# A new order of VectorE and ScalarE work in the paged-attention stage, with page numbers read ahead of the slot wait

## The reference

```python
q, k, v, c_in = split(u)                      # 8 heads; two score maps per head
# group A, samples: keys and values of 2048 past tokens come in pages of 128 tokens
k_past = cache_k[page_table]                  # (8 samples, 16 pages, 128 tokens, 8 heads, 128)
v_past = cache_v[page_table]
w = softmax(s_map1) - lam * softmax(s_map2)   # ALiBi bias in s
out = w_past @ v_past + w_new @ v_new         # then per-head RMSNorm
# group A, prompt: the same with causal blocks of 128 queries
# group B: GLU, causal depthwise convolution with 31 taps, LayerNorm over groups of 128 channels, swish
y = silu(group_layer_norm(conv31(a * sigmoid(g)) + b_dw))
h = h + concat(A, B) @ W_out
```

## Time and profile before

| | |
|---|---|
| median of 3 runs | 2753.17 us (2752.34 to 2759.67) |
| the profiled execution | 2753.05 us; its span 2751.3 us |
| PE busy | 2630.3 us (96%) |
| DVE, ACT, POOL busy | 1496.8, 943.5, 360.2 us |
| stage with K, V and S | about 1066 to 1553 us of the span |

### The profile page before, as it was taken

How to read it: one execution, slowest core, us unless ns; L and a number is a source line. 1 busy time by engine, 2 the same in 40 slices (tenths; PEclk the granted TensorE clock), 3 DMA queues, 4 the chain that set the end, 5 groups by cost and what they waited for, 6 DMA issues and landing times.

```text
span 2751.3 us, 49983 instructions
## 1 busy us (share of the span) xinstructions
PE 2630.3 (96%) x20082; PEld 2554.1 (93%) x20082; DVE 1496.8 (54%) x2082; ACT 943.5 (34%) x1076; POOL 360.2 (13%) x630
## 2 busy tenths in 40 slices
PE   7999999999999999988787799999999999999997
PEld 7999999999999999866665699999999999999997
DVE  5555555555555644376667345555555555555655
ACT  5222222222222422344445533222222222222443
POOL 2000000000000300165758010000000000000223
PEclk9999999999999999999899999999999999999998
DMA  5444434444444456798899944444444444444342
GB/s 230 151 153 152 145 145 152 152 149 143 150 152 147 142 192 221 287 339 325 315 334 352 363 157 152 154 149 149 146 152 152 146 146 151 152 146 145 140 150 83
DMA packets 92111, 506.36 MB, mean 184 GB/s; under 512 B 10401, under 2 KB 10402, under 8 KB 51298
## 3 DMA queue, kind: packets, MB, share of 16 engines
q1 hardware_dynamic: 90866, 496.59, 49.9%
q0 software_dynamic: 1136, 8.32, 0.8%
HBM read 495.63 MB, written 9.23 MB: 184 GB/s over the span
## 4 chain that ended last, share of the span: by engine, by line
PE 85%; DMA 4%; DVE 3%; ACT 3%; issue 2%; SPq 2%; POOL 1%; POOLq 0%; DVEq 0%; ACTq 0%
PE bank L1536 26%; PE bank L1538 26%; PE bank L1537 26%; DMA raw<-k_pool 2%; PE bank L1622 2%; PE bank L1624 2%; PE bank L1623 2%; POOL ssq L513 1%; SPq L423 1%; PE bank L1662 1%; SPq L424 1%; DMA raw<-slabs_out 1%; ACT x_hi L661 1%; PE bank L1688 1%; DVE y_c L1282 1%
## 5 line engine op out<-in xcount | busy, mean ns | idle before, releaser
L1536 PE MATMUL bank<-x_hi,w_hi 128*128 128x320 f32 x3584 | 1111.5, 310 | 17.7 <-DVE w_lo L1028 10.8
L1538 PE MATMUL bank<-x_hi,w_lo 128*128 128x320 f32 x3584 | 1110.0, 310 | 0.0
L1537 PE MATMUL bank<-x_lo,w_hi 128*128 128x320 f32 x3584 | 1109.9, 310 | 0.0
L1019 DVE TENSOR_TENSOR w_lo<-raw,w_hi 128x2048 fp32r<-128x2048 f32 x309 | 707.7, 2290 | 306.0 <-ACT w_hi L643 290.8
L643 ACT CAST w_hi<-raw 128x2048 fp32r<-128x2048 f32 x294 | 559.5, 1903 | 838.3 <-PE bank L1538 838.3
L1536 PEld LDWEIGHTS bank<-x_hi,w_hi 128*128 128x128 f32 x3584 | 675.2, 188 | 19.7 <-issue 13.5
L1537 PEld LDWEIGHTS bank<-x_lo,w_hi 128*128 128x128 f32 x3584 | 675.0, 188 | 0.2
L1538 PEld LDWEIGHTS bank<-x_hi,w_lo 128*128 128x128 f32 x3584 | 674.9, 188 | 0.0
L1536 PE MATMUL bank<-mid_hi,w_hi 128*128 128x320 f32 x1408 | 435.3, 309 | 1.0 <-DVE w_lo L1019 1.0
L1538 PE MATMUL bank<-mid_hi,w_lo 128*128 128x320 f32 x1408 | 435.1, 309 | 0.0
L1537 PE MATMUL bank<-mid_lo,w_hi 128*128 128x320 f32 x1408 | 435.1, 309 | 0.0
(11 more groups left out here) (216 smaller groups left out, 2040.1 us busy)
## 6 DMA issues: line engine op xcount, KB each, us to landing
raw<-slabs_ffn SPq DMA_DIRECT2D x264, 1024.0 KB, 4.8
raw<-k_pool SPq DMA_DIRECT2D x128, 512.0 KB, 6.5
raw<-v_pool SPq DMA_DIRECT2D x128, 512.0 KB, 5.7
raw<-slabs_in SPq DMA_DIRECT2D x48, 512.0 KB, 6.9
raw<-slabs_ple SPq DMA_DIRECT2D x18, 1024.0 KB, 4.8
raw<-slabs_in SPq DMA_DIRECT2D x16, 1024.0 KB, 4.8
raw<-slabs_out SPq DMA_DIRECT2D x16, 1024.0 KB, 4.9
h<-x_t SPq DMA_DIRECT2D x4, 640.0 KB, 8.1
```

The lines of the kernel that those rows point to most:

```text
L1019: vt.tensor_tensor(w_lo[n % 2][:, :, :], raw[n % 4][:, :].rearrange("p (k n) -> p k n", n=P), w_hi[n % 2][:, :, :].bitcast(F32), ALU.subtr ...
L1536: mm(out, w_hi[w2][:, t, :], xh, start=start, stop=False)
L1537: mm(out, w_hi[w2][:, t, :], xl, start=False, stop=False)
L1538: return mm(out, w_lo[w2][:, t, :], xh, start=False, stop=stop)
```

## The change

SP: `numbers` reads both page numbers of a slot before `slot_free` waits; the two transfers follow the wait. ACT: the high parts come before `copy_ET` (both in kind 2, the first one in kind 0), the second one of kind 0 before `head_exps`; a table load for the sigmoid stands ahead of the wait for its input; with q = 0 the exponentials come before `copy_ET`. DVE: a separate order for each kind, splits ahead of `head_read`, taps in groups of 2 to 6, `read_value` and `read_gate` ahead of the last group; `taps` are cut 8, 9 and 14 over kinds 2, 0 and 1 where they were cut 11, 10 and 10. PE: `combine` moves behind the first half, and in kind 2 `score_new` behind `weigh`. No instruction of DVE and PE is added or taken away, and one table load of ACT goes.

```diff
-            def two_pages(pool, b, g, slot):
-                for e in range(2):
-                    at = PAGES * b + 2 * g + e
-                    page = sp.value_load(page_row[0:1, at:at + 1], min_val=0, max_val=NPOOL - 1)
+            def numbers(at):
+                return [sp.value_load(page_row[0:1, 2 * at + e:2 * at + e + 1], min_val=0, max_val=NPOOL - 1)
+                        for e in range(2)]
+            def two_pages(pool, pages_, slot):
+                for e, page in enumerate(pages_):
                     sp.dma_start(ring[slot][:, 1024 * e:1024 * e + 1024],
...
-                slot_free(n, 1)
...
-                    two_pages(k_pool if kind == "K" else v_pool, at // KV_SLOTS, at % KV_SLOTS, slot)
+                    pages_ = numbers(at)
+                    slot_free(n, 1)
+                    two_pages(k_pool if kind == "K" else v_pool, pages_, slot)
... (ACT)
+                    if r == 0 and c < 8:
+                        half_up(2 * (9 + 2 * c))
+                    if r == 2 and c + 1 < 8:
+                        slab_up(8 + 2 * (c + 1))
+                    if q == 0:
+                        exp_scores(b, groups)
+                        if r == 0 and c < 8:
+                            half_up(2 * (9 + 2 * c) + 1)
                     copy_ET(b, q)
...
-                    if q < GROUPS - 1:
-                        exp_scores(b, ((1, 4), (2,), (3,))[q])
+                    if q:
+                        exp_scores(b, groups)
+                        if r == 0 and c < 8:
+                            half_up(2 * (9 + 2 * c) + 1)
                     if r == 0 and c < 8:
-                        half_up(2 * (9 + 2 * c))
                         head_exps(c)
-                        half_up(2 * (9 + 2 * c) + 1)
                     if r == 1:
                         if c < 8:
                             head_copy(c)
+                        if c - 2 < 8:
+                            sigmoid_tables()
...
-                    if r == 2:
-                        if c + 1 < 8:
-                            slab_up(8 + 2 * (c + 1))
... (DVE: the body of the quarter is replaced; kind 1 is)
+                    if r == 1:
+                        if c < 8:
+                            head_weights(c)
+                        if 0 <= c - 1 < 8:
+                            taps(c - 1, 17, 20)
+                        if q == 0 and b:
+                            out_store(b - 1)
+                        if it < NB:
+                            read_scores(it, q)
+                        if 0 <= c - 1 < 8:
+                            taps(c - 1, 20, 26)
+                        if last and it < NB:
+                            inverse_sums(b)
+                            read_new(it)
+                            maxima(it)
+                        if 0 <= c - 1 < 8:
+                            taps(c - 1, 26, 28)
+                        if c < 8:
+                            read_gate(c)
+                        if 0 <= c - 1 < 8:
+                            taps(c - 1, 28, TAPS)
... (PE)
-                    if q == 0 and b:
-                        combine(b - 1)
                     if r == 2 and 0 <= c - 1 < 8:
                         conv_mean(c - 1)
...
                     if q == 0:
+                        if b:
+                            combine(b - 1)
                         turn(b, q)
```

More of the change, by code:

```diff
@@ L731, in exp_tables, with sigmoid_tables @@
                 nc.scalar.preload_act_table_set("natural_log_exp_and_others")
+            def sigmoid_tables():
+                nc.scalar.preload_act_table_set("sigmoid_and_others")
             def half_up(n):
@@ L895, in _ @@
                     c, r = position(it, q)
+                    groups = ((1, 4), (2,), (3,), ())[q]
                     if q == 0 and b:
@@ L919, in _ @@
                             conv_sigmoid(c - 2)
-                        exp_tables()
-                    if r == 2:
-                        if c + 1 < 8:
-                            slab_up(8 + 2 * (c + 1))
-                        if 0 <= c - 1 < 8:
-                            conv_root(c - 1)
+                        if c - 2 < 8:
+                            exp_tables()
+                    if r == 2 and 0 <= c - 1 < 8:
+                        conv_root(c - 1)
                     if (it, q) == (NB - 1, 0):
@@ L1405, in _ @@
                             glu(c)
[L1406 to L1423, removed]
+                        if c + 1 < 8:
+                            half_low(2 * (10 + 2 * c))
                         if 0 <= c - 1 < 8:
@@ L1426, in _ @@
                         if c + 1 < 8:
[L1427 to L1440, removed]
+                            half_low(2 * (10 + 2 * c) + 1)
+                        if q == 0 and b:
+                            out_store(b - 1)
+                        if it < NB:
+                            read_scores(it, q)
+                        if c < 8:
+                            taps(c, 0, 4)
+                        if last and it < NB:
+                            inverse_sums(b)
+                            read_new(it)
+                            maxima(it)
+                        if c < 8:
+                            taps(c, 4, 8)
+                    if last and it == NB:
+                        inverse_sums(b)
                     if (it, q) == (NB - 1, 0):
@@ L1816, in _ @@
                         conv_half(halves[1])
-                    if q == GROUPS - 1 and it < NB:
+                    if q == GROUPS - 1 and it < NB and r < 2:
                         score_new(it)
@@ L1823, in _ @@
                     weigh(b, q)
+                    if q == GROUPS - 1 and it < NB and r == 2:
+                        score_new(it)
                     if q == 1:
```

21 lines of the change are left out of this document (20 added, 1 removed).

## The result

The changed kernel takes 2711.6 us (median of four runs, 2709.0 to 2719.17), the kernel before 2753.03 us on the same chip. The measured ratio, by which all that follows is compared, is 0.9837, 95% interval 0.9822 to 0.9852; the quotient of the two medians, 0.9850, lies inside the interval. The profiled execution took 2711.31 us with a span of 2709.5 us. That is 41.7 us less than the profiled execution before; the forecast was 29.4 us less.

A forecast was written before the change was run, and what follows sets the result against it. Paged stage near the transfer rate but not held by it: A held by transfers, C by PE's work and waits. 0.8 + 3.0 + 0.4 = 4.2 us per block, 29.4 us over seven, from 2753.05 to 2724 us; range 2704 to 2747.

The forecast's parts named there:

- much: Rival, chance 0.10: with slots freed early the ring runs at 399 GB/s; 38.5 us per block, 49 us less, 2704.
- C: Stretch from kind-0 `weigh` to kind-1 `weigh`, 17.8 us per block; claimed 14.8, 3.0 us less, with splits earlier.
- the floor: PE's own work in C: 12.7 us at full clock plus about half a microsecond, taken as 13.2 us.
- The bound of 4.6 us: The most C was said to lose per block, reached if it fell to the floor.
- A: Stretch from kind-1 `weigh` to the end of kind-0 `score`, 18.2 us per block; page numbers take 0.8 us off.
- what is added: Costs of the new order on ACT and DVE (later `copy_ET`, more taps in kind 1), counted as nothing.
- B: Rest of the block between A and C, 9.5 us; 0.4 us less, from late V in some blocks.
- Little: Rival, chance 0.14: the V slot then waits for `weigh`, only page numbers pay; 2740 to 2747 us, middle 2744.
- The slower one: Rival, chance 0.09: DVE's tail before `conv_mean` ends 7 us late, PE stands still, A grows; 2771 us.

The follow-up runs named there:

- the early `weigh`: Changed kernel with PE's `weigh` of a kind-1 quarter moved ahead of that quarter's second half, q = 0 to 3: ratio to before 0.9818 (2709.0 us).

## Why the prediction was right or wrong

**The time.** 2711.6 us lies in the range and on the predicted side, and inside the forecast's own 2710 to 2740, but at its edge. It is 12.4 us from the forecast's 2724 and 7.6 us from the 2704 of "much": in size that rival came nearer. Its mechanism is half seen: the ring runs at 358 to 392 GB/s per block, not yet at the 406 of the stage's end, and the block is 39.7 us where the forecast had 41.3 and "much" 38.5.

**C, the term that was mis-sized.** Predicted 3.0 us less, measured 5.0; seven times 2.0 us are 14 us, more than the whole miss of 11.3 us in the seven blocks. The step that failed is "I take 13.2 us as the floor and leave 1.6 us for waits that stay and for time at the lower of the two levels". Hardly a wait stayed (0.2 us in seven stretches), and no time at the lower level. The floor was too high as well: PE is busy for 12.7 us of C on the mean. That this is the sum of the pieces without the half microsecond added to it is luck: the pieces overlap (`weigh` starts at 1322.37 and lasts 1.95 us, `score` starts at 1324.14), and the barest stretch, without `weigh_new`, `score_new` or `combine`, takes 12.0 us (1302.80:1314.80 above); such work in the other stretches makes up the 0.7 on the mean. The bound of 4.6 us was therefore too small by 0.4. Of the 5.0 us, 14.44 - 12.72 = 1.7 are PE's busy time: C now lies at granted clock 1.00 throughout, where the prediction kept some time at the lower level.

**C, the reason.** The prediction gave SP's waits for splits as the reason why V and K come late and C is long. The waits did fall nearly as foretold (79.3 to 21.3 us, foretold under 20), and the early splits alone do take C from 17.8 to 13.8 us. But the waits alone do not hold C: with both splits late and the rest of the change in place they are 79.8 us, and C is 13.2. Then they hold A, by 1.3 us. What held C in the kernel before were several things for which PE stood still: V and K (9.5 us), `read_value` (8.5 us) and 7.1 us more. The prediction had `read_value` in the sum, "not counted again", as a part of the same 3.0 us; in truth the change without early splits is worth as much as the early splits alone, 32 us each. Which of its edits does that on the kernel before (`read_value` ahead of the taps, other bank reads, the rest of DVE's and ACT's order) was not tried apart and stays open.

**A.** Predicted 0.8 us less, from the page numbers; measured 0.4. On the kernel before the numbers alone gave 0.4 in A, and C grew by more; leaving them out of the changed kernel makes A 0.6 longer. Either is read from one execution, and neither is clear of noise in the time. The wait for `weigh` that was said to stay or grow grew, from 35.5 to 46.8 us: SP now arrives at it earlier. New, and counted as nothing in "what is added", is the 2.8 us for which `turn` waits twice for exponentials; the prediction followed `copy_ET` and `conv_mean` there and left out `exp_scores` of q = 0.

**B, `combine`.** Predicted 0.4 and 0; measured 0.3 to 0.4 and 0. The table loads were not tried apart; the trace before has ten pairs of them in the stage, not nine, which changes nothing in the sum.

**The rivals.** "Little" is out: SP's waits for splits fell and the block with them; its price for the numbers alone, 7 x 0.8 us, was too high, as the ratio of 0.9994 shows. The slower one did not come: in the changed kernel PE waits at `conv_mean` only once, for 1.3 us, and that behind POOL's part of `y_c`, which the prediction did not follow, and not behind DVE's taps; DVE is busy for 9.9 of C's 12.8 us. With the early `weigh` DVE's sum does hold PE, for 3.3 us. The Trainium skill (SBUF — State Buffer, Who interferes with whom) says that a VectorE instruction with two SBUF inputs contends with a GpSimd instruction that reads SBUF. The trace agrees: in the seven blocks of the changed kernel POOL's first instruction of a step (L603) takes 0.62 us at the median beside such a VectorE instruction, and 0.45 us otherwise. But packing DVE's work into less time added no cost here: DVE is busy for 30.90 us per block against 30.81, and POOL for 202.7 us in the seven blocks against 207.2.

## What to carry to other kernels

When several waits hold the same stretch of the engine that sets the pace, taking out one half of them or the other can give nearly the same gain, and both together less than the sum: so price the stretch by what that engine needs with no wait at all, not by the sum of the waits that an edit removes. A wait on a queue costs only where the waited-for data is then needed: SP's 80 us for splits, against 21, cost 13 us, and in another stretch than the prediction had put them. Once a stretch has no gap, count its matmuls at the full clock, from start to start and not by lengths that overlap, and look for the next gain where the engine still stands still, here by freeing the next slots earlier.

## What the runs showed of the hardware

Two fifths of the gain, 15.9 of the 40.7 us of the seven blocks, is PE's busy time, which I read as the clock. In C the granted clock is 1.00 in all seven stretches where PE has no gap, and 0.73 to 0.91 in six of the seven of the kernel with the numbers alone, in which PE stands still for 131.4 - 108.8 = 22.6 us:

```profile
1230.00:1246.10 16.10, 13.70 (x188) 11.45 (x187) 12.78 (x33) 2.44 (x5) 12.80 (x29) 1.00 0.96 360
...
sum 131.40, PE 108.81 PEld 90.58 DVE 92.75 ACT 34.39 POOL 84.87; mean PE 15.54 PEld 12.94 DVE 13.25 ACT 4.91 POOL 12.12
```

Of these seven, the row shown is the one at 1.00. Stretches with gaps can thus cost twice, in idle time and in longer matmuls. But not every gap goes with a lower clock: the fourth A of the kernel with both splits late, shown above, has 5.9 us in which PE stands still, at granted clock 1.00. That the gaps themselves bring the clock down was not tried by itself.
